# Credits after the first loads, a split wait for the first key copies, and another order on VectorE in the last pair of heads

## The reference, cut to what matters

```python
# SEQ = D_MODEL = 1024, 16 heads of 64
def neighborhood_attention(x, w_qkv, rpb, w_o):
    qkv = (x @ w_qkv).reshape(bsz, rows, GRID_W, 3, NA_HEADS, HEAD_DIM)
    q = qkv[:, :, :, 0] * HEAD_DIM ** -0.5
    ...
    s = jnp.where(col_in[:, None, :], s + bias, -jnp.inf)      # 8 x 16 neighbours of each query
    pr = jax.nn.softmax(s, axis=(-2, -1))
    return jnp.einsum('bhqak,bakhd->bqhd', pr, v_b)            # then @ w_o

for i in range(DEPTH):                                         # DEPTH = 1
    x = layer_norm(DN_ALPHA * x + mix, ln1_g[i], ln1_b[i])
    hid = jnp.square(jax.nn.relu(x @ w_ff1[i]))
    ple = jax.nn.sigmoid(x @ w_ple_gate[i]) * (p[i] @ w_ple_proj[i])
    x = layer_norm(DN_ALPHA * x + hid @ w_ff2[i] + ple, ln2_g[i], ln2_b[i])
```

## Time and profile before

| | |
|---|---|
| median of 3 runs | 1226.57 us (1225.44 to 1226.8) |
| the profiled execution | 1225.39 us, span of its trace 1223.2 us |
| mean granted PE clock | 0.998 |
| PE busy | 1212.9 us, 99% |
| DVE busy | 883.4 us, 72% |
| ACT busy | 593.2 us, 48% |
| DMA queue q1 | 53.9% of 16 engines' span |
| chain that ended last | PE 97%, DMA 1%, DVE 1%, ACT 1%, issue 1% |

### The profile page before, as it was taken

One profiled execution on the slowest core, in us unless ns is written; L12 is line 12 of the kernel. 1 busy time (PEld: TensorE's weight loads), 2 busy tenths in 40 slices (PEclk: granted clock), 3 DMA queues, 4 the chain that ended last, 5 costly groups with the idle time before them and its releaser, 6 DMA issues.

```text
span 1223.2 us, 17908 instructions
## 1 busy us (share of the span) xinstructions
PE 1212.9 (99%) x5820; PEld 1019.5 (83%) x5820; DVE 883.4 (72%) x1743; ACT 593.2 (48%) x1144; POOL 103.9 (8%) x71
## 2 busy tenths in 40 slices
PE   9999999999999999999999999999999999999997
PEld 7888888888888888888888888888888888888886
DVE  3777677777777867769677777776764575588786
ACT  3555655655556843244444444444453433333671
POOL 0212222122123004200000000000000000000000
PEclk9999999999999999999999999999999999999999
DMA  8332223213233758683556566565569776768633
GB/s 220 82 76 70 58 72 89 55 55 75 55 106 85 273 158 233 211 285 117 192 207 240 177 220 219 184 239 179 219 238 381 279 273 222 259 232 316 191 104 103
DMA packets 162726, 215.61 MB, mean 176 GB/s; under 512 B 11488, under 2 KB 91232, under 8 KB 162272
## 3 DMA queue, kind: packets, MB, share of 16 engines
q1 hardware_dynamic: 162656, 214.72, 53.9%
HBM read 147.44 MB, written 58.90 MB: 169 GB/s over the span
## 4 chain that ended last, share of the span: by engine, by line
PE 97%; DMA 1%; DVE 1%; ACT 1%; issue 1%; SPq 0%; DVEq 0%; ACTq 0%
PE bank L2771 25%; PE bank L2739 25%; PE bank L1218 19%; PE bank L1371 7%; PE bank L2695 6%; PE bank L1324 4%; PE bank L1301 3%; PE bank L1280 3%; PE bank L1256 2%; PE bank L1362 1%; PE bank L1234 1%; PE bank L258 1%; PE bank L1272 0%; DMA k_lo_twice<-k_lo_twice 0%; DMA x_chunk<-in_x 0%
## 5 line engine op out<-in xcount | busy, mean ns | idle before, releaser
L879 ACT ACTIVATE probabilities<-negated_scores,negated_max 128x384 f32<-128x384 f32 (+1 forms) x128 | 75.6, 590 | 136.7 <-DVE negated_max L1095 136.4
L1218 PE MATMUL bank<-act_T_hi,w_qkv_hi 128*128 128x512 f32 x336 | 133.5, 397 | 0.0
L1218 PE MATMUL bank<-act_T_lo,w_qkv_hi 128*128 128x512 f32 x336 | 133.5, 397 | 0.0
L1218 PE MATMUL bank<-act_T_hi,w_qkv_lo 128*128 128x512 f32 x336 | 131.9, 393 | 0.0
L2739 PE MATMUL bank<-x_combination,weight_parts 128*128 128x512 f32 x504 | 118.5, 389 | 0.0
L1076 DVE TENSOR_TENSOR prob_T_lo<-bank,prob_T_hi 128x256 fp32r<-128x256 f32 (+2 forms) x160 | 69.1, 448 | 58.4 <-ACT prob_T_hi L870 56.8
L2739 PEld LDWEIGHTS bank<-x_combination,weight_parts 128*128 128x128 f32 x504 | 94.6, 188 | 19.6
L2739 PE MATMUL bank<-act_T_hi,weight_parts 128*128 128x512 f32 x240 | 77.3, 389 | 0.0
L2099 ACT ACTIVATE hidden_staging<-hidden_staging 128x512 f32<-128x512 f32 x48 | 30.3, 632 | 95.0 <-DVE hidden_staging L2436 95.0
L770 POOL TENSOR_TENSOR w_qkv_lo<-weight_raw,w_qkv_hi 128x1024 fp32r<-128x1024 f32 x21 | 50.3, 2394 | 294.4 <-ACT w_qkv_hi L825 294.4
L2771 PE MATMUL bank<-x_combination,hidden_parts_odd 128*128 128x512 f32 (+1 forms) x324 | 73.1, 381 | 0.0
(11 more groups left out here) (263 smaller groups left out, 2803.5 us busy)
## 6 DMA issues: line engine op xcount, KB each, us to landing
hidden_combinations<-hidden_staging SPq DMA_DIRECT2D x112, 256.0 KB, 2.5
w_ff_in<-in_w_ff SPq DMA_DIRECT2D x27, 1024.0 KB, 7.8
weight_raw<-in_w_ff SPq DMA_DIRECT2D x25, 1024.0 KB, 5.7
weight_raw<-hidden_combinations SPq DMA_DIRECT2D x14, 1024.0 KB, 5.4
hidden_in<-hidden_combinations SPq DMA_DIRECT2D x14, 1024.0 KB, 5.6
weight_raw<-in_na_w_qkv SPq DMA_DIRECT2D x21, 512.0 KB, 4.4
bias_in<-rpb_rows SPq DMA_DIRECT2D x256, 6.0 KB
attention_T<-out_T SPq DMA_DIRECT2D x8, 512.0 KB, 3.2
```

The costliest lines, as they stand in the source:

```text
L879: nc.scalar.activation(prob[:, u % 4, 0:n], score[:, u % 2, 0:n], ACT.Exp, scale=-1.0, bias=nmax[:, u % 4:u % 4 + 1], accum_out=total[:, u ...
L1218: mm = nc.tensor.matmul(proj_ps[gi % 2][:, :], w[wp][:, (par + kind) % 2, k, :], S.act[ap][:, k, t * HALF:(t + 1) * HALF], start=(i == 0), ...
```

## The change

Four edits:

1. SP adds its credits after the eight chunks, not before the first; DVE writes the zeros before its seven credits, not after; PE adds its two credits after the first idle products.
2. The copies of the first keys: `k_doubled` now counts the two DMAs of head 0's first half alone (a credit of 32 stands for the other two, so that the counts of later pairs stay as they were), and the wait of step 3 counts the other six.
3. In the last pair, in the steps that follow a `wo_low` or the low part of attention rows, DVE does `turned_tile(s-4)` first, ahead of add_bias(s) and normalise(s-2). With a `turned_tile` to do, these are steps 5, 7, 8, 10, 11, 15, 17, 18 and 19; the last two have neither add_bias nor normalise, so nothing changes in them.
4. Names and blank lines.

```diff
@@ k_half_twice
+                    done = k_second_doubled if t or h else k_doubled
...
-                                     k_st[part][own, 0, h, cols].bitcast(F32)).then_inc(k_second_doubled if t else k_doubled, 16)
+                                     k_st[part][own, 0, h, cols].bitcast(F32)).then_inc(done, 16)
@@ sync
-            sp.sem_inc(out_stored, 16)
-            for kind in (K_, Q_):
-                sp.sem_inc(S.raw_in[kind], 16)
+            def credits():
+                sp.sem_inc(out_stored, 16)
+                sp.sem_inc(k_doubled, 32)
+                for kind in (K_, Q_):
+                    sp.sem_inc(S.raw_in[kind], 16)
...
                 load_first_w(k)
+            credits()
             sp.wait_ge(w_first_in, 16)
@@ vector
+            nc.vector.memset(score[:, 0, 0:P], 0.0).then_inc(first_q, 1)
             for credit, n in ((proj_free, 4), (score_done, 2), (turned_lo, 2), (out_done, 2), (y_free, 4),
                               (o_lo, 2), (w_lo, 3)):
                 dve.sem_inc(credit, n)
-            nc.vector.memset(score[:, 0, 0:P], 0.0).then_inc(first_q, 1)
@@ vector, body
+                    late = not more and (s - 2 in WO_SPLIT_STEP or s - 1 in EARLY_LOW_STEP)
+                    if late and PARTS <= s < UNITS + PARTS:
+                        turned_tile(j, s - PARTS)
                     if not more and s < UNITS:
                         add_bias(j, s)
                     if NORMAL <= s < UNITS + NORMAL:
                         normalise(j, s - NORMAL)
-                    if PARTS <= s < UNITS + PARTS:
+                    if not late and PARTS <= s < UNITS + PARTS:
                         turned_tile(j, s - PARTS)
@@ tensor
                 if u == 3:
-                    pe.wait_ge(k_second_doubled, 64)
+                    pe.wait_ge(k_second_doubled, 96)
...
-            pe.sem_inc(y_full, 4)
...
-            pe.sem_inc(pv_done, 3)
             pe.wait_ge(first_q, 1)
             idle_products(WARM[0])
+            pe.sem_inc(y_full, 4)
+            pe.sem_inc(pv_done, 3)
```

More of the change, by code:

```diff
@@ L384, in attention @@
         k_doubled = sem("k_doubled")
-        k_second_doubled = sem("first_k_second_half_doubled")
+        k_second_doubled = sem("rest_of_first_k_doubled")
         v_turned = sem("v_turned")
```

## The result

The changed kernel takes 1230.12 us (median of 7 runs, 1229.4 to 1230.6). The kernel before took 1225.71 in 7 runs beside them (1225.1 to 1226.8). The ratio is 1.0035, with an interval from 1.0025 to 1.0044: slower by 4.4 us, or 0.35%. The profiled executions differ by 4.0 us (1229.4 and 1225.39, spans 1227.2 and 1223.2).

The account below looks back on a forecast made before the run. PE, busy 1212.9 of 1223.2 us, was taken as the bound, with DVE and ACT leading in the last pair. -0.2 - 0.55 + 3.5 = +2.75 us on 1226.57 gave 1229.3 us, 8 in 10 from 1226.9 to 1231.1.

Parts of the forecast that it names:

- Part 3: Last pair: DVE's new order delays steps 5, 7, 8, 10, 11 and 15, adding up to 3.5 us lost (2.8 to 4.0).
- Rival B: Last pair: DVE's waits for ACT are not there, only steps 5, 8, 11 cost, 1.33 us; 1227.2 us; chance 0.13.
- rival C: Last pair: not slower, PE is released by the low parts alone and gains some 0.5 us; 1225.3 us; chance 0.07.
- Part 2: First score product: no longer held by the fourth key copy; gain 0.55 us (0.4 to 0.6).
- Part 1: Start: moved credits bring SP's first loads and the first product 0.20 us earlier; gain 0.2 us (0 to 0.3).
- rival D: Start: the pause after the earlier idle products puts off the clock's rise, 1.8 us more; 1231.1 us; chance 0.10.
- The signs: Trace: first product 0.2 us earlier, first score 0.7 to 0.8 earlier; last pair: DVE waits, longer ACT waits, more PE idle.
- The sign for a late clock: Start: transposes at the low clock level beyond 7 us would show the forecast wrong.

Follow-up runs that it names:

- a gain of 1.2 for the other: Against the kernel before: key edit, and in the last pair `wo_low` moved behind the next step's bias (the opposite order); 1223.86 us, 0.9987.

## Why the prediction was right, and where not

**The time.** 1229.3 was forecast and 1230.12 came. Part of that closeness is luck: the forecast stood on a median of 1226.57 for the kernel before, and seven runs gave 1225.71. The effect is +4.4 us, where the sum was +2.75; a base that was 0.9 too high made up for half of the difference. Slower by over 0.2% was the likeliest side, and is what came.

**Part 3, +3.5: right.** 3.6 us in all three traces with the order, and step by step 0.48, 0.88, 0.53, 0.82, 0.33 and 0.5 where the sum had 0.48, 0.82, 0.5, 0.77, 0.35 and 0.58. The reading that carried it was that in steps 5, 8 and 11 ACT waits for DVE's maximum, so that what stands ahead of the bias is paid in full, and in 7, 10 and 15 DVE comes to the low part before ACT does. DVE's waits were forecast as 0.82, 0.77 and 0.58 and are 0.78, 0.72 and 0.55. Rival B (no such waits; 1.33 us) falls by these rows, and rival C (PE is released by the low parts alone) by PE's waits, which are now named after the scaled probabilities, 0.9 us in three.

**Part 2, -0.55: mis-sized.** The profiled pair shows the 0.55 (it is 0.57 there), but so do the kernels that keep the old wait. The step that failed took the 5.00 us of one copy as the copies' time and only tested that even with it the new wait passes. It did not ask how often the old wait holds PE: one trace in five. The term is nearer -0.1.

**Part 1, -0.2: not borne out.** The prices of the credits were right (SP 0.20, the zeros 0.65 earlier). The gain of 0.20 at the transposes was 0.07 in the profiled execution and 0.13 in the mean, and the first product waits for later inputs that scatter by 1.6 us. Against that stands the clock, which rival D had put at 0.10: in the changed kernel's trace it rose 2.4 us later, and the products from 9.92 on came 0.98 later. So the mechanism of rival D was at work in this trace. Its price of 1.8 was too high: of the 0.98, 0.46 stand at the first product, behind idle products that run to 7.78, and 0.52 in the three products that start ahead of the rise (7.43, 8.00 and 8.43). By the medians the credits cost 0.15 (alone) to 0.6 us (with the keys, 1225.92 against 1225.32), both within their intervals, so that not even the sign is sure.

**The sum again.** 3.6 - 0.1 + 0.15 to 0.6 is 3.65 to 4.1 us, against 4.4 between medians and 4.0 between profiles. The 0.3 to 0.75 that are left to the medians lie well inside the interval of the difference, 3.1 to 5.4 us; medians of the kernel before alone lie between 1225.50 and 1225.80 in five comparisons. Whether there is more to it than this scatter stays open.

**The signs.** The waits of DVE, ACT's longer waits and the new name in PE's waits came. PE's idle time between 400 and 445 us grew by 1.75 us (0.43 before, 2.18 after), where 2 to 3 were named; the rest of the 3.6 shows only in the starts of the matmuls, whose ends are modelled. The first product came 0.46 later (7.43 against 6.97) instead of 0.2 earlier, and the first score, free of the copy as forecast, 0.51 later than 49.41 instead of 0.7 to 0.8 earlier. The sign for a late clock named transposes at the low level beyond 7 us. It was idle products, and the first three products by the weights, that were started there.

## What to carry to other kernels

On an engine's in-order queue, put first what another engine waits for, and what waits for another engine as late as it can stand: here the same rule forecast a loss of 3.5 us for one order and a gain of 1.2 for the other, and both came (3.6 and 1.5). A hold that hangs on one transfer's time, and a clock that rises at its own moment, must be read from several executions before they become terms of a sum.

## What the runs showed of the hardware

The moment at which the clock rose, with the same instructions ahead of it, lay between 5.41 and 8.26 us in six executions, and the matmul of 9.92 moved by up to 1.1 us with it (-0.12 to 0.95), of which the late weights have a part. In the executions with the earliest rises, at 4.70, 5.29 and 5.41, nothing came of them: the first product waited for the weights until 7.01, 7.21 and 7.14. The same copy of 128 KB, the fourth of the first keys, took between 2.70 and 5.00 us to land in 14 executions of 14 kernels.
